# Feed-forward stage of a hybrid decoder layer: two-by-two block products with seven products in place of eight

## The chip, the core and the metric

One core of one Trainium2 chip runs the whole kernel. The metric is device time in microseconds (us), the median of the runs. TensorE does the matmuls, VectorE (DVE), ScalarE (ACT) and GpSimd (POOL) work elementwise, SyncE (SP) issues nearly all DMAs.

## What is computed

One decoder layer: a mixer (attention and a state-space part), then a gated feed-forward with a causal convolution of width 3 over the tokens. 2048 prompt tokens and 8 sample tokens; model width 1024, hidden width 2816, all float32. The part that matters:

```python
xn = rmsnorm(x, p['g_pre_ffn'])
gate = xn @ p['w_gate']
up = xn @ p['w_up']
padded = jnp.concatenate([conv_prev.astype(gate.dtype), gate], axis=1)
conv = p['conv_b'] + sum(padded[:, i:i + t] * cw[i] for i in range(CONV_W))
hdn = jax.nn.gelu(conv) * up
x = x + rmsnorm(hdn @ p['w_down'], p['g_post_ffn'])
```

## The kernel before

Stages follow each other: projections and state-space part, attention, the mixer's output projection (`stage_mix`), the feed-forward (`stage_ffn`). Each float32 matmul is made of three passes: an operand is split into a high part (a copy to type fp32r, on ScalarE, "hi") and the rest (a subtraction on VectorE, "lo"), and hi x hi, hi x lo and lo x hi are summed in PSUM. One such pass is one matmul instruction of 128x128 weights and 512 columns.

The feed-forward works on four blocks of 512 tokens (`CH`). In each block, 22 channel tiles of 128 hidden channels (`FT`) are made one after the other: `channels` (L2496) makes gate, then up, 8 slices of the model width x 3 passes = 24 matmuls each. ScalarE copies gate out of PSUM (L2647) and splits the next tile's weights (L2612); VectorE subtracts (L2705), runs the three taps (L2735, L2738), multiplies by up (L2760) and splits the hidden tile (L2765). The hidden block stays in SBUF (`hh`, `hl`). Then the block's down projection (L2598) goes over the 22 channel tiles, for four token tiles of 128 and two halves of the output width: 22 x 4 x 2 x 3 = 528 matmuls in 8 PSUM banks. The norm and the residual end each block. `w_gate` and `w_up` are read once per block, so is `w_down`. The order is written out by hand, each engine's in its own function, tied by semaphores: an engine that waits holds all that is queued behind it.

`ffn_ahead` holds the buffers that `stage_mix` fills before the feed-forward begins: x of the first block and the weights of the first tile are split there, and `ffn_first` (L2232) makes the first gate and up tile at the end of `stage_mix`. The eight sample tokens go through in the last block (L2515, L2524, L2540), beside the prompt's work.

## Time and profile before

| what | value |
|---|---|
| runs | 3451.25, 3447.12, 3445.88 us; median 3447.12 |
| profiled execution | span 3451.6 us; no time of its own is listed beside the three runs |
| mean granted TensorE clock | 0.974 |
| TensorE busy | 3242.8 us, 94% |
| VectorE, ScalarE, GpSimd busy | 2044.9, 1320.9, 603.7 us |
| HBM | 506.91 MB read, 59.30 MB written |

The feed-forward stage takes the end of the span, from 1930 us. The sum of the prediction is made against the span; the median of the runs is 4.5 us (0.13%) below it. A line such as L2496 is a line of the kernel; "idle" in a group is the time that its engine stood still just before those instructions. A matmul's mean duration is its latency: matmuls overlap, so the pace is read from counts in a window.

### The profile page before, as it was taken

The numbers are of one execution on the slowest core, as the hardware profiler recorded it, in microseconds if no ns is written. First come the engines' busy times: TensorE is split into PE (matmuls) and PEld (weight loads), VectorE is DVE, ScalarE is ACT, GpSimd is POOL, SyncE is SP. The second block draws the span as 40 slices with busy tenths as digits, with TensorE's granted clock in tenths as the row PEclk, the third lists the DMA queues.
The fourth block names the chain that finished last, engine by engine and source line by source line (L and its number), as shares of the span: only waits on it lengthen the run. The fifth ranks groups of instructions, "written<-read, shape, count | busy, mean of one in ns | idle before, by whom it ended". The sixth has DMA issues, their size and how long they took to land. (4 is left out here: it accounts for less than half of the span.)

```text
span 3451.6 us, 48037 instructions
## 1 busy us (share of the span) xinstructions
PE 3242.8 (94%) x14753; PEld 2237.2 (65%) x14753; DVE 2044.9 (59%) x2786; ACT 1320.9 (38%) x2177; POOL 603.7 (17%) x618
## 2 busy tenths in 40 slices
PE   6999885999999999998899999999999999999998
PEld 5787753444334344343788688788878887877776
DVE  6110677987988988994566555345543554255532
ACT  4100113566566556563444333223322333233321
POOL 2000101643444444441144000000000000000000
PEclk9999987999999999999899999999999999999999
DMA  3322234978988988986556333433343334344333
GB/s 116 98 79 67 77 90 111 302 239 279 303 277 284 304 276 289 306 302 235 175 167 180 99 95 109 140 110 98 97 153 105 98 98 143 101 135 122 111 118 116
DMA packets 489476, 569.78 MB, mean 165 GB/s; under 512 B 62896, under 2 KB 310800, under 8 KB 487613
## 3 DMA queue, kind: packets, MB, share of 16 engines
q1 hardware_dynamic: 482190, 551.61, 51.2%
q10 hardware_dynamic: 6912, 15.26, 1.4%
q8 instruction: 90, 1.47, 0.2%
q14 instruction: 108, 0.88, 0.1%
q0 software_dynamic: 176, 0.56, 0.1%
HBM read 506.91 MB, written 59.30 MB: 164 GB/s over the span
## 5 line engine op out<-in xcount | busy, mean ns | idle before, releaser
L2496 PE MATMUL tail_bank<-ahead_xh,ahead_wh 128*128 128x512 f32 x1392 | 547.3, 393 | 3.9 <-DVE ahead_wl L2705 2.5
L2496 PE MATMUL tail_bank<-ahead_xl,ahead_wh 128*128 128x512 f32 x1392 | 542.7, 390 | 0.0
L2496 PE MATMUL tail_bank<-ahead_xh,ahead_wl 128*128 128x512 f32 x1392 | 542.4, 390 | 0.0
L2705 DVE TENSOR_TENSOR ahead_wl<-ahead_stage,ahead_wh 128x1024 fp32r<-128x1024 f32 x173 | 211.9, 1225 | 357.2 <-ACT ahead_wh L2612 357.0
L1374 POOL TENSOR_TENSOR att_S<-att_S,att_X 128x512 f32<-128x512 f32 (+3 forms) x256 | 345.2, 1348 | 284.3 <-PE att_bank L1663 221.8
L1558 DVE TENSOR_TENSOR att_prod<-att_Kr,att_q_wide 128x1024 f32<-128x1024 f32 x256 | 325.9, 1273 | 4.9 <-DMA att_Kr<-in_cache_k_dram 4.6
L1658 PE MATMUL att_bank<-att_X,att_negtri 128*128 128x512 f32 (+3 forms) x640 | 297.2, 546 | 31.3 <-DVE att_X L1529 30.7
L1563 DVE TENSOR_REDUCE att_z_s<-att_prod 128x16 f32<-128x1024 f32 x256 | 313.2, 1224 | 8.8
L2496 PEld LDWEIGHTS tail_bank<-ahead_xh,ahead_wh 128*128 128x128 f32 x1392 | 261.7, 188 | 67.2 <-issue 11.2
L2709 DVE TENSOR_TENSOR ffn_wdl<-ahead_wdf,ffn_wdh 128x1024 fp32r<-128x1024 f32 x88 | 107.5, 1225 | 332.0 <-ACT ffn_wdh L2617 331.9
L2496 PEld LDWEIGHTS tail_bank<-ahead_xh,ahead_wl 128*128 128x128 f32 x1392 | 261.7, 188 | 55.1
L2496 PEld LDWEIGHTS tail_bank<-ahead_xl,ahead_wh 128*128 128x128 f32 x1392 | 262.0, 188 | 53.1
L1424 ACT ACTIVATE att_X<-att_bank 128x512 f32<-128x512 f32 (+2 forms) x320 | 171.1, 535 | 257.2 <-PE att_bank L1647 219.5
L1663 PE MATMUL att_bank<-att_S,att_negones 128*128 128x512 f32 (+3 forms) x576 | 257.6, 529 | 0.0
L2598 PE MATMUL tail_bank<-ffn_wdh,ffn_hh 128*128 128x512 f32 x704 | 217.7, 391 | 16.5 <-issue 8.7
L2617 ACT ACTIVATE ffn_wdh<-ahead_wdf 128x1024 fp32r<-128x1024 f32 x88 | 92.8, 1058 | 339.6 <-PE tail_bank L2598 312.0
L1432 ACT ACTIVATE att_Wt<-att_bank 128x512 f32<-128x512 f32 (+2 forms) x320 | 168.8, 527 | 127.7 <-PE att_bank L1663 127.6
L2598 PE MATMUL tail_bank<-ffn_wdh,ffn_hl 128*128 128x512 f32 x704 | 216.9, 389 | 0.0
L2598 PE MATMUL tail_bank<-ffn_wdl,ffn_hh 128*128 128x512 f32 x704 | 216.9, 389 | 0.0
L2458 POOL TENSOR_TENSOR ffn_st<-ffn_st,kept_eps 128x1 f32<-128x1 f32 x16 | 4.9, 304 | 1170.1 <-ACT ahead_stage L2691 1073.9
L1529 DVE SCALAR_TENSOR_TENSOR att_X<-att_X,att_bank 128x512 f32<-128x512 f32 (+2 forms) x320 | 190.9, 599 | 27.9 <-ACT att_X L1426 27.0
L1647 PEld LDWEIGHTS att_bank<-att_qhh,att_khl 128*128 128x128 f32 x320 | 60.9, 190 | 217.0 <-ACT att_Wt L1432 137.8
(395 smaller groups left out, 5611.3 us busy)
## 6 DMA issues: line engine op xcount, KB each, us to landing
att_Kr<-in_cache_k_dram SPq DMA_DIRECT2D x512, 256.0 KB, 3.8
att_Vr<-in_cache_v_dram SPq DMA_DIRECT2D x488, 256.0 KB, 3.8
ahead_wdf<-in_w_down_dram SPq DMA_DIRECT2D x108, 512.0 KB, 3.5
ahead_stage<-in_w_gate_dram SPq DMA_DIRECT2D x89, 512.0 KB, 3.9
ahead_stage<-in_w_up_dram SPq DMA_DIRECT2D x88, 512.0 KB, 3.9
qku_work<-in_x_prompt_dram SPq DMA_DIRECT2D x16, 512.0 KB, 4.0
norm_xr<-in_x_prompt_dram SPq DMA_DIRECT2D x16, 512.0 KB, 4.2
x_dram<-norm_y SPq DMA_DIRECT2D x16, 512.0 KB, 4.8
```

The costliest lines, as they stand in the source:

```text
L1374: pool.tensor_tensor(new[:, r:], old[:, r:], x[:, r:], ALU.add).then_inc(s_part, 1)
L1424: act.activation(x, bank[:, s % NZ, cols(s):], ACT.Exp).then_inc(e_ready, 1)
L1432: act.activation(Wt[:, u % NW, cols(u):], bank[:, u % NZ, cols(u):], ACT.Exp).then_inc(w_ready, 1)
L1529: stt(x, x, LN_TOP, z, ALU.min, ALU.max).then_inc(sp_ready, 1)
L1558: tt(pr, Kr[:, kk % KSLOTS], q_wide[:, None, :].to_broadcast([P, PP, AW]), ALU.mult).then_inc(k_used, 1)
L1563: dve.tensor_reduce(z_s[:, :, kk * PP:(kk + 1) * PP].rearrange("p h r -> p r h"), prod[:, kk % 2, :].rearrange("p (k h d) -> p k h d", k=P ...
L1658: last = pe.matmul(bank[:, u % NZ, o:], negtri[:], X[:, u % NX, o:], start=False, stop=True, skip_group_check=True)
L1663: last = pe.matmul(bank[:, u % NZ, o2:], negones[:], S[:, (u - 1) % 2, o2:], start=False, stop=True, skip_group_check=True)
L2496: mm = pe.matmul(bank[:, first + f % 2, :], w[:, j, k, :], x[:, k, :], start=(k == 0 and n == 0), stop=(k == KD - 1 and n == 2))
L2598: mm = pe.matmul(bank[:, 2 * t + c, :], x[:, f, cols], w[:, sl, c * CH:(c + 1) * CH], start=(f == 0 and n == 0), stop=(f == FT - 1 and n = ...
L2705: tt(wl[:, j], wf[:, j], wh[:, j].bitcast(F32), ALU.subtract).then_inc(w_lo[j], 1)
L2709: tt(wdl[:, f % 2, :], wdf[:, f % 2, :], wdh[:, f % 2, :].bitcast(F32), ALU.subtract).then_inc(wd_lo, 1)
```

## The change

A product of two-by-two blocks is made from seven block products in place of eight, with sums of blocks before and after.

**Gate and up.** The four weight blocks are gate and up (rows) by the two halves of the model width; the four x blocks are the halves of the model width by two halves of 512 tokens out of a pass of 1024 (`PASS`). The stage makes two passes over the 22 channel tiles, 44 tiles `g` (`LASTG`). Each makes seven products K1, K6, K2, K7, K5, K4, K3 in this order, each of 4 slices x 3 passes = 12 matmuls (L2689), into the PSUM banks A, B and C, two sets of three. K2, K7, K4 and K3 add onto what a bank holds, and wait until the sum before has been read: K2 for ScalarE's copy `m1`, K7, K4 and K3 for VectorE's sums `u2`, `u3` and `c22`. GpSimd makes four weight sums a tile (`weight_sums`), ScalarE and VectorE split seven weight operands of 512 columns a tile in place of two of 1024. The x operands of seven products, hi and lo, stay in SBUF. For pass 0 they are made at the head of the stage from `xnT` (`split_q`, operands of 128x2048); for pass 1 GpSimd's `sum_parts` sums quarters in tiles 4 to 19 and stores them to a DRAM tensor `xsum`; 28 slices are loaded and split during tile 21.

**Hidden.** For every two tiles GpSimd makes five sums of hidden blocks (`sum_h`), and seven operands are stored to the DRAM tensor `hop`, 256 KB each.

**Down.** The hidden channels are paired even and odd, the output width and the tokens halved. Seven products of eight steps each (56 steps `s`); a step is 11 pairs x 3 = 33 matmuls, and its left operand (128x1408) is loaded from `hop` and split by ScalarE and VectorE, two buffers. The right operands, 11 per product, are loaded through a ring of three buffers (`NWD`), summed by GpSimd (`sum_wd`), split (`split_wd`). VectorE and ScalarE add the products up in SBUF (`gather`, `evacuate`). Norm and residual follow in products 4 and 6.

**In `stage_mix`** x is no longer prepared, the first seven weight operands are (with GpSimd's sums), and `ffn_first` is gone.

```diff
+def weight_sums(pool, early, s, n, which):
+    wf, S, w_sum, tt = early["wf"], early["S"], early["w_sum"], pool.tensor_tensor
+    for j in which:
+if j:
+    pool.wait_ge(w_sum, n * 4 + j)
+if j == 0:
+    tt(S[:, 0], wf[:, s, A21], wf[:, s, A22], ALU.add).then_inc(w_sum, 1)
+elif j == 1:
+    tt(S[:, 1], S[:, 0], wf[:, s, A11], ALU.subtract).then_inc(w_sum, 1)
+elif j == 2:
+    tt(wf[:, s, A21], wf[:, s, A11], wf[:, s, A21], ALU.subtract).then_inc(w_sum, 1)
+else:
+    tt(wf[:, s, A12], wf[:, s, A12], S[:, 1], ALU.subtract).then_inc(w_sum, 1)
...
-        def one_block(b, last, begun=False):
-                    for n, (w, x) in enumerate(((wh, xh), (wh, xl), (wl, xh))):
-                        mm = pe.matmul(bank[:, first + f % 2, :], w[:, j, k, :], x[:, k, :],
-                                       start=(k == 0 and n == 0), stop=(k == KD - 1 and n == 2))
-                mm.then_inc(done, 1)
...
+        def product(g, k, s, first):
+            pe.wait_ge(w_lo, g * OPS + k + 1)
+            b = 3 * s + (A_B, B_B, A_B, B_B, C_B, B_B, C_B)[k]
+            if k in (K1, K6, K5):
+                at(pe, {K1: c11_ready, K6: c21_ready, K5: c12_ready}[k], g - 1)
+            else:
+                pe.wait_ge({K2: m1_ready, K7: u2_ready, K4: u3_ready, K3: c22_ready}[k], g + 1)
+            for q in range(KH):
+                if first == 0 and q == 0:
+                    pe.wait_ge(x_ready[k], 1)
+                if first == 1:
+                    pe.wait_ge(x_ready[k], 2 + q)
+                for n, (w, x) in enumerate(((0, 0), (0, 1), (1, 0))):
+                    mm = pe.matmul(bank[:, b, :], wop[:, k, w, q], xop(k, x)[:, q], start=(k in (K1, K6, K5) and q == 0 and n == 0),
+                                   stop=(q == KH - 1 and n == 2), skip_group_check=True)
+            mm.then_inc(prod, 1)
...
-                    for n, (x, w) in enumerate(((hh, wdh), (hh, wdl), (hl, wdh))):
-                        for c in range(2):
-                            mm = pe.matmul(bank[:, 2 * t + c, :], x[:, f, cols], w[:, sl, c * CH:(c + 1) * CH],
-                                           start=(f == 0 and n == 0), stop=(f == FT - 1 and n == 2))
...
+        for s in range(LASTS):
+            i, u = divmod(s, STEPS)
...
+            pe.wait_ge(a_lo, s + 1)
+            if s < 3:
+                pe.wait_ge((c11_ready, c21_ready, c12_ready)[s], LASTG - 1)
+            else:
+                at(pe, c_act, act_reads(s - 3))
+                at(pe, c_dve, dve_reads(s - 3))
+            for p in range(PAIRS_F):
+                n = i * PAIRS_F + p
+                if u == 0:
+                    pe.wait_ge(wd_lo, n + 1)
+                for q, (a, w) in enumerate(((0, 0), (0, 1), (1, 0))):
+                    mm = pe.matmul(bank[:, s % 3, :], a_op[s % 2][a][:, p, :], wd_op[:, n % NW, w, :], start=(p == 0 and q == 0),
+                                   stop=(p == PAIRS_F - 1 and q == 2), skip_group_check=True)
+                if u == STEPS - 1 and p < PAIRS_F - 1:
+                    mm.then_inc(wd_used, 1)
+            mm.then_inc(acc, 1)
...
+        def prepare(g, s, h2):
+            for j in range(2):
+                pool.wait_ge(w_loaded[j][s], h2 * 16 + 16)
+            if known(g, FT):
+                pool.wait_ge(s_made, g - FT + 1)
+            pool.wait_ge(w_lo, g * OPS - OPS + K5 + 1)
+            weight_sums(pool, early, s, g, (0, 1, 2))
+        def finish(g, s):
+            pool.wait_ge(w_lo, g * OPS + K2 + 1)
+            weight_sums(pool, early, s, g, (3,))
+        def sum_h(g, j, h2):
+            pool.wait_ge(h_ready, g)
+            e, o = conv[:, (j - 2) % 4], conv[:, (j - 1) % 4]
+            for x, a, b, op in ((0, e[:, 0:CH], o[:, 0:CH], ALU.add), (1, e[:, CH:], o[:, CH:], ALU.add),
+                                (2, e[:, 0:CH], o[:, CH:], ALU.add), (3, o[:, 0:CH], o[:, CH:], ALU.subtract)):
+                at(pool, hsum_stored[x], h2 * (32 if x == 0 else 16) - (32 if x == 0 else 16))
+                tt(hsum[:, x, :], a, b, op).then_inc(hsummed, 1)
+            pool.wait_ge(hsum_stored[0], h2 * 32 - 16)
+            tt(hsum[:, 0, :], e[:, CH:], e[:, 0:CH], ALU.subtract).then_inc(hsummed, 1)
...
+        def sum_parts(i, c):
+            n = i * 2 - 2 + c
+            pool.wait_ge(xp_loaded, n * 64 + 64)
+            for x, (o, a, b) in enumerate(((0, 1, 0), (1, 3, 1), (3, 3, 0), (2, 2, 3))):
+                if x:
+                    pool.wait_ge(xt_made, n * 4 + x)
+                tt(parts[:, o], parts[:, a], parts[:, b], ALU.subtract).then_inc(xt_made, 1)
+        def body(g, j, h2, i=None):
+            if not known(g, LASTG - 1):
+                prepare(g + 1, (j + 1) % 2, h2 + j % 2)
+            if known(g, 0, 1):
+                pool.wait_ge(x_ready[K2], 1)
+                pool.wait_ge(x_sum, 2)
+                tt(xq[:, 2], xq[:, 2], xq[:, 3], ALU.subtract).then_inc(x_t4, 1)
+            if j % 2 == 0 and not known(g, 0, 1):
+                sum_h(g, j, h2)
+            if i is not None and j % 2 == 0:
+                sum_parts(i, j // 2)
+            if not known(g, LASTG - 1):
+                finish(g + 1, (j + 1) % 2)
...
+        def body(g, f, j, h2):
+            s = j % 2
+            turn = known(g, FT - 1, FT)
+            sampled = known(g, FT - 1, LASTG - 1)
+            last = known(g, LASTG - 1)
+            for k in range(OPS):
+                if k == K1:
+                    act.wait_ge(prod, g * OPS + k + 1)
+                    at(act, c21_ready, g)
+                    if known(g, 0, 1):
+                        act.wait_ge(x_t4, 1)
+                        act.wait_ge(x_ready[K6], 1)
+                    act.activation(m1, bank[:, 3 * s + A_B, :], ACT.Copy).then_inc(m1_ready, 1)
+                    if known(g, 0, 1):
+                        split_q(K4, 2, x_t4, 1)
+                if k == K2:
+                    act.wait_ge(prod, g * OPS + k + 1)
+                    at(act, tapped, g * CW)
+                    act.activation(gbuf[:, CW - 1:CW - 1 + CH], bank[:, 3 * s + A_B, :], ACT.Copy).then_inc(c11_ready, 1)
+                if not last:
+                    split(g + 1, k, (j + 1) % 2, h2 + j % 2)
+                else:
+                    for n in ((0, 1), (2, 3), (4, 5), (6, 7), (8, 9), (10,), ())[k]:
+                        split_wd(n)
+                    if k == K2:
+                        split_a(0)
...
+            at(dve, saved, g)
+            ts(gbuf[:, 0:CW - 1], tl[:, 0:CW - 1], 1.0, None, ALU.mult).then_inc(carried, 1)
+            dve.wait_ge(carried, g + 1)
+            dve.wait_ge(c11_ready, g + 1)
...
+                dve.wait_ge(x_ready[K3], 1 + KH)
+            ts(c, gbuf[:, 0:PASS], tap(0), p[:, BIAS:], ALU.mult, ALU.add).then_inc(tapped, 1)
+            for k in (1, 2):
+                dve.wait_ge(tapped, g * CW + k)
+                stt(c, gbuf[:, k:k + PASS], tap(k), c, ALU.mult, ALU.add).then_inc(tapped, 1)
+            ts(tl[:, 0:CW - 1], gbuf[:, PASS:], 1.0, None, ALU.mult).then_inc(saved, 1)
...
+            for k in range(OPS):
+                if k in (K6, K7, K5, K4, K3):
+                    dve.wait_ge(prod, g * OPS + k + 1)
+                if k == K6:
+                    dve.wait_ge(m1_ready, g + 1)
+                    at(dve, tapped, g * CW)
+                    at(dve, saved, g)
+                    tt(t1, m1, b(B_B), ALU.add).then_inc(u2_ready, 1)
+                if k == K7:
+                    at(dve, h_ready, g)
+                    if known(g, 0, 1):
+                        dve.wait_ge(x_t4, 1)
+                    tt(up[:, CH:], m1, b(B_B), ALU.add).then_inc(u3_ready, 1)
+                if k == K5:
+                    dve.wait_ge(u3_ready, g + 1)
+                    tt(up[:, CH:], up[:, CH:], b(C_B), ALU.add).then_inc(c22_ready, 1)
+                if k == K4:
+                    dve.wait_ge(c22_ready, g + 1)
+                    tt(up[:, 0:CH], m1, b(B_B), ALU.add).then_inc(c21_ready, 1)
+                if k == K3:
+                    dve.wait_ge(u2_ready, g + 1)
+                    tt(t1, t1, b(C_B), ALU.add).then_inc(c12_ready, 1)
+                    taps(g, f, j, h2)
+                if not last:
+                    split(g + 1, k, (j + 1) % 2)
+                else:
+                    for n in ((), (0, 1), (2, 3), (4, 5), (6, 7), (8, 9), (10,))[k]:
+                        split_wd(n)
+                    if k == K7:
+                        split_a(0)
+                    if k == K3:
+                        split_a(1)
+                if k == K6 and not known(g, 0, 1):
+                    multiply(g - 1, (j - 1) % 4)
+                if k == K7 and sampled:
+                    sample_taps(g - FT + 1)
+                if k == K4 and sampled:
...
+        def load_wd(n):
+            i, p = divmod(n, PAIRS_F)
+            at(sp, wd_lo, n - NWD + 1)
+            for h, (odd, d) in enumerate(PAIRED[i]):
+                r = (2 * p + odd) * P
+                sp.dma_start(wd_raw[n % NWD][:, h], A["w_down"][0, r:r + P, d * CH:(d + 1) * CH]).then_inc(wd_loaded[n % NWD], 16)
...
+            if g == LASTG - 1:
+                sp.wait_ge(w_lo, LASTG * OPS)
+                sp.wait_ge(s_made, FT)
+                sp.wait_ge(x_ready[K3], 1 + KH)
+                for x in range(2):
+                    sp.wait_ge(hraw_stored[x], 16 * PAIRS_F)
+                for x in range(4):
+                    sp.wait_ge(hsum_stored[x], 16 * PAIRS_F * (2 if x == 0 else 1))
+                load_wd(0)
+                load_wd(1)
+                load_a(0)
+                load_wd(2)
+                load_a(1)
+                for n in range(NWD, PAIRS_F):
+                    load_wd(n)
+            if g % 2 == 0 and g:
+                store_h(g, (g - 2) % FT, g % 4, g // 2)
+            if g == FT - 1:
+                for n in range(NX):
+                    load_x(n)
+        for g in range(4):
...
+                ("hop", [OPS * T // 2, FT // 2 * P]), ("xsum", [4 * KH * P, CH])):
```

Order on VectorE, one gate/up tile before (512 tokens of gate and up, half of what a tile of the change makes):

```order
L2730 TENSOR_SCALAR ffn_gbuf<-ffn_tails 128x2
L2735 TENSOR_SCALAR ffn_conv<-ffn_gbuf,ahead_prm 128x512
L2738 SCALAR_TENSOR_TENSOR ffn_conv<-ffn_gbuf,ahead_prm,ffn_conv 128x512 x2
L2739 TENSOR_SCALAR ffn_tails<-ffn_gbuf 128x2
L2760 TENSOR_TENSOR ffn_conv<-ffn_conv,tail_bank 128x512
L2705 TENSOR_TENSOR ahead_wl<-ahead_stage,ahead_wh 128x1024
L2765 TENSOR_TENSOR ffn_hl<-ffn_conv,ffn_hh 128x512
L2705 TENSOR_TENSOR ahead_wl<-ahead_stage,ahead_wh 128x1024
```

And in the change, from the sum `u3` (L3033) of one tile to the sum `u2` (L3025) of the next:

```order
L3033 TENSOR_TENSOR gate_work<-gate_work,tail_bank 128x512
L2938 TENSOR_TENSOR ahead_wop<-ahead_S,ahead_wop 128x512
L3036 TENSOR_TENSOR gate_work<-gate_work,tail_bank 128x512
L2938 TENSOR_TENSOR ahead_wop<-ahead_wf,ahead_wop 128x512
L3039 TENSOR_TENSOR gate_work<-gate_work,tail_bank 128x512
L2984 TENSOR_SCALAR gate_work<-ffn_tails 128x2
L2995 TENSOR_SCALAR gate_work<-gate_work,ahead_prm 128x1024
L2998 SCALAR_TENSOR_TENSOR gate_work<-gate_work,ahead_prm 128x1024 x2
L2999 TENSOR_SCALAR ffn_tails<-gate_work 128x2
L2938 TENSOR_TENSOR ahead_wop<-ahead_wf,ahead_wop 128x512 x2
L3025 TENSOR_TENSOR gate_work<-gate_work,tail_bank 128x512
L2938 TENSOR_TENSOR ahead_wop<-ahead_S,ahead_wop 128x512
```

The taps, now 1024 wide, stand between the sum that ends a tile (L3039) and the sum `u2` (L3025) that the next tile's K7 waits for; the two splits behind them (L2938 x2) are those of K3 and K1.

Order on GpSimd in two tiles of gate/up (before, the engine had nothing there):

```order
L1731 TENSOR_TENSOR ahead_S<-ahead_wf 128x512
L1733 TENSOR_TENSOR ahead_S<-ahead_S,ahead_wf 128x512
L1735 TENSOR_TENSOR ahead_wf<-ahead_wf 128x512
L1737 TENSOR_TENSOR ahead_wf<-ahead_wf,ahead_S 128x512
L1731 TENSOR_TENSOR ahead_S<-ahead_wf 128x512
L1733 TENSOR_TENSOR ahead_S<-ahead_S,ahead_wf 128x512
L1735 TENSOR_TENSOR ahead_wf<-ahead_wf 128x512
L2594 TENSOR_TENSOR gate_work<-gate_work 128x512 x4
L2596 TENSOR_TENSOR gate_work<-gate_work 128x512
L1737 TENSOR_TENSOR ahead_wf<-ahead_wf,ahead_S 128x512
```

L2594 and L2596 are `sum_h`, L1737 is the fourth weight sum; it stands behind `sum_h`, and in tiles 4 to 19 behind `sum_parts` too.

Order on ScalarE in the last gate/up tile (g = 43):

```order
L2849 ACTIVATE gate_work<-tail_bank 128x512
L2814 ACTIVATE ffn_xw<-ahead_S 128x512
L2814 ACTIVATE ffn_xw<-ahead_wf 128x512
L2814 ACTIVATE ffn_xw<-ffn_stage 128x512
L2814 ACTIVATE ffn_xw<-ahead_S 128x512
L2797 ACTIVATE gate_work<-gate_work 128x1024
L2855 ACTIVATE gate_work<-tail_bank 128x512
L2814 ACTIVATE ffn_xw<-ahead_wf 128x512
L2814 ACTIVATE ffn_xw<-ffn_stage 128x512
L2822 ACTIVATE ahead_wop<-ahead_wf 128x1408
L2814 ACTIVATE ffn_xw<-ahead_S 128x512
L2814 ACTIVATE ffn_xw<-ahead_wf 128x512
```

L2814 splits right operands of down, L2797 is the gelu of tile 42, L2822 the first left operand. L2849 is the copy `m1`.

## Rows read from the trace of the kernel before

**Rows 1.** The page: span, TensorE's busy time, then GB/s in 40 equal slices of the span.

```profile
span 3451.6 us, 48037 instructions
PE 3242.8 (94%) x14753; PEld 2237.2 (65%) x14753; DVE 2044.9 (59%) x2786; ACT 1320.9 (38%) x2177; POOL 603.7 (17%) x618
GB/s 116 98 79 67 77 90 111 302 239 279 303 277 284 304 276 289 306 302 235 175 167 180 99 95 109 140 110 98 97 153 105 98 98 143 101 135 122 111 118 116
```

**Rows 2.** Windows: matmuls of L2496 alone; window, length, PE busy, PEld busy, granted clock, DMA.

```profile
2380.00:2500.00 120.00, 120.00 (x531) 99.36 (x530) 1.00 0.33 97
```

**Rows 3.** The page's groups of instructions: matmuls; out<-in, shapes, count, busy us, mean ns, idle.

```profile
L2496 PE MATMUL tail_bank<-ahead_xh,ahead_wh 128*128 128x512 f32 x1392 | 547.3, 393 | 3.9 <-DVE ahead_wl L2705 2.5
L2598 PE MATMUL tail_bank<-ffn_wdh,ffn_hh 128*128 128x512 f32 x704 | 217.7, 391 | 16.5 <-issue 8.7
```

**Rows 4.** The same groups from 1960 us on: TensorE's work for the eight sample tokens.

```profile
L2515 PE MATMUL tail_bank<-ahead_stage,ffn_xs 128*32 128x256 f32 (+1 forms) x352 | 24.3, 396 | 5.6 <-issue 5.0 <-DVE ffn_hs L2757 0.6
L2524 PE MATMUL tail_bank<-kept_sel,ffn_s_rows 128*128 128x8 f32 x88 | 11.2, 237 | 0.0
L2540 PE MATMUL tail_bank<-ahead_wdf,ffn_hs 128*32 128x512 f32 x80 | 10.7, 605 | 0.0
```

**Rows 5.** Waits of TensorE from 1930 us on: total, times, longest.

```profile
PE tail_bank L2598 <- issue: 8.7, 4, 2.6
PE tail_bank L2598 <- DVE ffn_wdl L2709: 7.7, 3, 3.1
```

**Rows 6.** Timeline of TensorE, 1920 to 1940 us: start, duration, instruction, idle time before.

```profile
1920.33 1.02 PE L2190 MATMUL tail_bank<-kept_ident,norm_xn 8*128 8x8 f32 x8 [2.56 <-DVE norm_xn L2166]
1925.29 0.63 PE L2232 MATMUL tail_bank<-ahead_xh,ahead_wh 128*128 128x512 f32 x1
1925.72 0.63 PE L2232 MATMUL tail_bank<-ahead_xl,ahead_wh 128*128 128x512 f32 x1
1930.69 0.47 PE L2496 MATMUL tail_bank<-ahead_xh,ahead_wh 128*128 128x512 f32 x1 [1.13 <-PEq L63]
1938.91 0.50 PE L2496 MATMUL tail_bank<-ahead_xh,ahead_wh 128*128 128x512 f32 x1 [2.50 <-DVE ahead_wl L2705]
```

**Rows 7.** Timeline of the DMA queue: the last issue of the stage before the feed-forward.

```profile
1921.70 0.37 SPq L1956 DMA_DIRECT2D xnT_dram<-norm_xt  x1
```

**Rows 8.** Timeline of VectorE within one gate tile.

```profile
2418.15 0.55 DVE L2735 TENSOR_SCALAR ffn_conv<-ffn_gbuf,ahead_prm 128x512 f32<-128x512 f32 x1 [0.28 <-DVE ffn_gbuf L2730]
2418.85 0.75 DVE L2738 SCALAR_TENSOR_TENSOR ffn_conv<-ffn_gbuf,ahead_prm,ffn_conv 128x512 f32<-128x512 f32 x1 [0.15 <-DVE ffn_conv L2735]
2422.16 1.22 DVE L2705 TENSOR_TENSOR ahead_wl<-ahead_stage,ahead_wh 128x1024 fp32r<-128x1024 f32 x1 [0.26 <-ACT ahead_wh L2612]
```

**Rows 9.** Groups from 1960 us on: an addition that reads PSUM, and ScalarE's split and PSUM copy.

```profile
L2760 DVE TENSOR_TENSOR ffn_conv<-ffn_conv,tail_bank 128x512 f32<-128x512 f32 x85 | 58.4, 687 | 37.8 <-ACT ffn_conv L2651 37.8
L2612 ACT ACTIVATE ahead_wh<-ahead_stage 128x1024 fp32r<-128x1024 f32 x168 | 176.0, 1048 | 0.0
L2647 ACT ACTIVATE ffn_gbuf<-tail_bank 128x512 f32<-128x512 f32 x85 | 51.0, 600 | 309.2 <-PE tail_bank L2496 309.2
```

**Rows 10.** GpSimd: one group by form; then a stretch of the timeline where it meets VectorE.

```profile
L1374 POOL TENSOR_TENSOR att_S<-att_S,att_X 128x512 f32<-128x512 f32 x168 | 264.9, 1577 | 284.3 <-PE att_bank L1663 221.8 <-DVE att_X L1529 62.6
...
1855.36 1.81 POOL L2023 TENSOR_TENSOR norm_sq<-norm_sq 128x512 f32<-128x512 f32 x1
1856.32 1.92 DVE L2107 TENSOR_TENSOR norm_mixl<-norm_mix,norm_mixh 128x1024 fp32r<-128x1024 f32 x1 [0.31 <-ACT norm_mixh L2050]
1857.24 1.60 POOL L2025 TENSOR_TENSOR norm_sq<-norm_sq 128x256 f32<-128x256 f32 x1
```

**Rows 11.** DMA issues of the page: KB each, median us from issue to landing.

```profile
ahead_stage<-in_w_gate_dram SPq DMA_DIRECT2D x89, 512.0 KB, 3.9
```

**Rows 12.** Timeline, the end: TensorE's last matmuls and the last addition.

```profile
3438.02 0.61 PE L2598 MATMUL tail_bank<-ffn_wdh,ffn_hl 128*128 128x512 f32 x2
3445.90 1.22 DVE L2801 TENSOR_TENSOR ahead_wdf<-ffn_sums,ahead_wdf 128x1024 f32<-128x1024 f32 x1
```

1140 lines of the change are left out of this document (613 added, 527 removed).

## The prediction, made before the changed kernel was run

> **What bounds the kernel now.** I read the page first, then windows and groups, then waits, then the timeline. TensorE is busy 94% of the span [rows 1]. From 1930 us on it is the bound: in a window of 120 us within gate and up it never stands still, at full granted clock, and makes 531 matmuls [rows 2], so one costs 120/531 = 0.226 us (the 0.39 us of its groups is latency, [rows 3]). Its waits in the whole stage are few: 8.7 and 7.7 us before the down matmuls [rows 5]. So a matmul that is left out is worth 0.226 us, as long as the other engines keep up, and the question is whether they do.
>
> **What is removed.** Gate and up took 4 x 22 x 48 = 4224 matmuls (three groups of 1392 and the first tile's 48, [rows 3]), and take 44 x 84 = 3696. Down took 3 x 704 = 2112, and takes 56 x 33 = 1848. The difference is 792, times 0.226 = 179 us. Shapes and columns stay the same. Weights are read twice, not four times; a 512 KB load lands in 3.9 us [rows 11], and per pair of tiles the new stage moves 2 MB of weights, 1.75 MB of `hop` and about 1 MB of x quarters in 38 us, 125 GB/s, well below the 300 GB/s that the page's slices show in attention [rows 1]. I cost the bytes at nothing; if a load is late it stands in the terms below.
>
> **The head of the stage.** Before, the last projection work hid x and the first tile. Now nothing of x can be loaded until `stage_mix` ends. Its last store is issued at 1921.7 [rows 7]; with a landing like that of a small transfer (under 3.9 us) and the 1.1 us which TensorE idled between the stages [rows 6], the new stage starts at about 1926. Then four loads of 1 MB: at 300 GB/s 3.4 us each, the first lands at +4.5, the last at +16. Operands of 2048 columns cost twice the rows for 1024: ScalarE 2.1 us [rows 9], VectorE 2.4 us [rows 8]. VectorE has K1's lo, a sum, the lo of K3 and K2 (+20.6, behind the last load), a second sum (23), then K6's lo behind ScalarE (27.5). So TensorE makes K1 at about +10 and K6 only at +27; three more lo parts, one weight split and `u2` put K7 at +35, and four products of 12 x 0.226 = 2.7 us follow: tile 0 is done at +46, at 1972 us. The bounds are 1962 (GpSimd and landings hidden) and 1987 (GpSimd's two 2048-wide sums at four times the 1.58 us of [rows 10] each in the chain).
>
> **A steady tile.** 84 x 0.226 = 19.0 us; 43 tiles are 816 us. VectorE per tile: 7 splits and 5 PSUM sums at 0.69 [rows 9], taps and product of 1024 columns at 1.08, 1.28, 1.28 and 1.22 (from 0.55, 0.75 and the 1024-wide split, [rows 8]; slopes of 0.53 us per 512), small ones 0.3: 13.5 us, and ScalarE about 6.6. Both fit in 19. But order matters. With time 0 at K1: K3 of the tile before has just ended (0.2), VectorE sums (0.9), carries two columns (1.3), runs three taps with the 0.15 to 0.28 us between dependent ones [rows 8] (5.7), splits K3 and K1 (7.0), and only then makes `u2` (7.8). K7 should start at 3 x 2.72 = 8.2. The margin is 0.4 us. `u3` and `c22` have 1.8 us.
>
> Two things eat that margin. First, GpSimd: an addition of 512 columns takes 1.58 us on average [rows 10], and where it meets VectorE both stretch: 1.92 in place of 1.22 for VectorE, 1.60 for GpSimd's 256 columns [rows 8, 10]. Per two tiles it has 8 weight sums and 5 hidden sums, 13 x 1.58 = 20 us of 38: it fits, but after `sum_h` the next tile's first three sums fall on the taps. Second, in tiles 4 to 19 the order weight sums, `sum_h`, `sum_parts`, fourth sum is serial: the product of the even tile is ready at 9, five sums end at 16 to 17, only then SP issues the loads of the quarters (land at 20.5), four sums of 256 (23.8), fourth weight sum (25.1). ScalarE waits for that in its split of K3, in front of `m1`: `m1` comes at 26.4, K2 should start at 24.5. So about 2.8 us for each odd tile of pass 0 (10 of them, 28 us) and 0.9 us for each of pass 1 (11, 10 us): **38 us**. The bounds are 0 (margins hold) and 120 us (below).
>
> The same lines as rule: the Trainium skill, SBUF — State Buffer, section Who interferes with whom, says that VectorE and GpSimd share a port pair as an exclusive lock, and that a VectorE instruction with two SBUF inputs fully blocks behind a GpSimd one that reads SBUF. The rows of the stretched pair agree in direction. By it both wide taps could each lose a whole GpSimd addition in every tile; that is the second rival, and speaks against this change.
>
> **Turn, transition, down.** In tile 21, 28 slices of x are split besides: 28 x 0.69 = 19 us more on VectorE, 33 in all against 19, of which about 9 can be taken from later slack (K7 of tile 22 starts at 35 and not at 27): **10 us** (0 to 19). In the last tile ScalarE's order has right operands of down before the gelu, and they come through a ring of three: load 3.5 to 3.9 us [rows 11], sum 1.3 to 1.6 [rows 10], hi and lo 0.6 and 0.7. SP may load only when tile 43's splits are done (+6), so ScalarE stands until about +12, VectorE reaches `u3` at +21 where K4 wanted it at +13.6, and the eleventh operand comes at about +42, when step 0 should have ended at +26.5: **20 us** with a slow clock behind it (bounds 5 and 35). Down itself is 1848 x 0.226 = 418 us; a step is 7.5 us, in which VectorE has a split of 1408 (1.7), one or two sums, 1.4 small splits and at most a norm and residual (2.5): under 6, hidden. **4 us** for waits where a product's last three right operands turn over (before, down waited 16 us in all, [rows 5], which bounds it). The sample tokens' work stays: 24.3 + 11.2 = 35 us in gate/up, 10.7 and some tails, 15 us, in down [rows 4]. After the last matmul: a sum 0.7, square 1.2, root 0.8, scale 1.3, add 1.2, store; the present end takes 3451.6 - 3438.6 = 13 us [rows 12], I take 10.5.
>
> **Sum:** 1972 + 816 + 35 + 38 + 10 + 20 + 418 + 15 + 4 + 10.5 = 3338.5 us of span, 113 below 3451.6. The median stands 4.5 below its span, so **3334 us**.
>
> **The rivals.**
> *Clean.* Margins hold, and the loads' latency is hidden: the 72 us of stalls are gone, 3262 us. For it: the trace shows loads landing early and few waits [rows 5, 11]. Against: three separate margins of about a microsecond. With half of the stalls, 3298.
> *GpSimd sets the chain.* Both wide taps wait a whole GpSimd addition (2 x 1.58) in every tile, `u2` comes at 11.0, 2.8 us late: 43 x 2.8 = 120 in place of 38, 3416 us. For it: the stretched pair [rows 10]. Against: only odd tiles have the sums there by my order.
> *Slow clock, slower than before.* Behind an idle of 2.56 us, twelve matmuls ran 0.43 us apart and not 0.226 [rows 6]: 2.4 us more, TensorE at the lower of its two levels. If every tile has a stall of 2.5 us and this tail, it is 4.9 x 43 = 211 in place of 38, 3507 us. It beats the gain from (3447 - 3334 + 38)/43 = 3.5 us a tile. Against: my stalls are shorter. I give it 8%.
> *Even.* Stalls of just this size, or products that are not paced as now: within 0.2% of before, which is about what a measurement can tell; 2%.
>
> **How the numbers follow.** Forecast 60%, clean 12%, GpSimd chain 18%, slow clock 8%, even 2%. The range runs from 3280 (half way into clean) to 3430 (the GpSimd chain with its 14 us of room); outside lie slow clock, even, and half of clean. Faster: 60 + 12 + 18 = 90%; same 2%; slower 8%.
>
> **What would show it.** In the new trace: L2689 with 3696 matmuls and down with 1848, at 0.226 us in windows without waits; the first K6 about 27 us after the stage's start; in odd tiles 5 to 19 TensorE idle before K2 for ScalarE's copy, and ScalarE idle before K3's split for L1737; TensorE idle before K7 for L3025; a gap of over 5 us in tile 43 and another in step 0. Wrong would be: windows in mid-stage with less than 80 matmuls per 19 us and no wait named (the clock), waits for DMA at L2689, or down steps far over 7.5 us.

## The result and the profile after

The changed kernel takes 3461.9 us (median of 19 runs, 3453.08 to 3472.53) against 3451.15 us (19 runs) for the kernel before in the same session: ratio 1.003, 95% interval 1.0021 to 1.0039. It is 0.3% slower. The prediction said 3334 us, with a range up to 3430: wrong in size and in direction. The profiled execution has a span of 3457.6 us and took 3459.6 us; the sum of the prediction stood at 3338.5 us of span, so 119 us are to be explained.

The page of the changed kernel, the lines that answer to [rows 1] and [rows 3]:

```profile
span 3457.6 us, 47005 instructions
PE 3148.2 (91%) x13945; PEld 2115.6 (61%) x13945; DVE 2335.3 (68%) x2904; ACT 1323.6 (38%) x2249; POOL 1179.2 (34%) x996
...
L2689 PE MATMUL tail_bank<-ffn_xw,ahead_wop 128*128 128x512 f32 x2112 | 530.4, 409 | 72.9 <-DVE ffn_xw L2943 31.6
L2766 PE MATMUL tail_bank<-ffn_xw,ahead_wop 128*128 128x512 f32 x1848 | 451.0, 405 | 20.8 <-DVE ahead_wop L2957 17.6
L2689 PE MATMUL tail_bank<-gate_xr,ahead_wop 128*128 128x512 f32 x1584 | 381.6, 399 | 16.2 <-DVE gate_work L3030 11.5
```

The counts are the announced ones: 2112 + 1584 = 3696 and 1848, 792 fewer than before. TensorE's busy time fell only by 95 us, from 3242.8 to 3148.2, where 792 x 0.2267 us are 180 us. And it now waits, where it had hardly waited [rows 5]. Waits of TensorE in the changed kernel from 1900 us on (total us, times, longest):

```profile
PE tail_bank L2689 <- DVE ffn_xw L2943: 31.6, 2, 17.8
PE tail_bank L2689 <- ACT gate_work L2849: 27.9, 8, 4.3
PE tail_bank L2766 <- DVE ahead_wop L2957: 17.6, 7, 4.4
PE tail_bank L2689 <- DVE gate_work L3030: 11.5, 2, 10.5
PE tail_bank L2689 <- DVE gate_work L3025: 8.9, 1, 8.9
...
PE tail_bank L2724 <- ACT down_C L2911: 7.4, 1, 7.4
```

The places are found in the timeline of TensorE, changed kernel (start, duration, instructions, idle before):

```profile
1936.91 5.46 PE L2689 MATMUL tail_bank<-ffn_xw,ahead_wop 128*128 128x512 f32 x12 [13.75 <-DVE ffn_xw L2943]
1960.21 7.18 PE L2689 MATMUL tail_bank<-ffn_xw,ahead_wop 128*128 128x512 f32 x24 [17.84 <-DVE ffn_xw L2943]
1979.25 2.03 PE L2689 MATMUL tail_bank<-ffn_xw,ahead_wop 128*128 128x512 f32 x8
...
2184.05 8.56 PE L2689 MATMUL tail_bank<-gate_xr,ahead_wop 128*128 128x512 f32 x36
2192.45 5.76 PE L2689 MATMUL tail_bank<-ffn_xw,ahead_wop 128*128 128x512 f32 x24
2201.55 7.42 PE L2689 MATMUL tail_bank<-ffn_xw,ahead_wop 128*128 128x512 f32 x24 [3.33 <-ACT gate_work L2849]
2208.80 8.56 PE L2689 MATMUL tail_bank<-gate_xr,ahead_wop 128*128 128x512 f32 x36
...
2433.15 3.33 PE L2689 MATMUL tail_bank<-ffn_xw,ahead_wop 128*128 128x512 f32 x7 [8.88 <-DVE gate_work L3025]
...
2926.78 5.46 PE L2689 MATMUL tail_bank<-gate_xr,ahead_wop 128*128 128x512 f32 x12 [10.51 <-DVE gate_work L3030]
...
2967.18 1.02 PE L2724 MATMUL tail_bank<-kept_ident,ffn_tails 128*10 128x128 f32 x4 [7.38 <-ACT down_C L2911]
...
3009.65 50.56 PE L2766 MATMUL tail_bank<-ffn_xw,ahead_wop 128*128 128x512 f32 x216
...
3268.86 1.65 PE L2766 MATMUL tail_bank<-ffn_xw,ahead_wop 128*128 128x512 f32 x3 [4.31 <-DVE ahead_wop L2957]
```

Two things are read here. First the **pace**: 36 matmuls from 2184.05 to 2192.45 without a gap, 8.40/36 = 0.2333 us each, at a granted clock of 1.00 (window 2184 to 2192); down has the same (216 in 50.56 us: 215 distances and the last one's 0.4 us). In the kernel before it is 0.2267 us: the window of [rows 2] counts 531, of which about 1.7 belong to its edges, 120/529.3. Over 5544 matmuls that is 5544 x 0.0066 = 37 us. Nothing waits there: it is a slower TensorE at the same clock, and no row of waits would show it. Second the **gaps**, and behind each a tail: the 24 matmuls after the gap at 2201.55 take 7.25 us to the next start where 24 took 5.6, 1.65 us more: the granted clock is 0.58 of full speed in the first 3.5 us of them and 0.94 in the next 4, so a part of them ran at the lower of the two levels, as in [rows 6].

Term by term against the prediction's sum (span; the tiles and steps are measured between the first matmuls of each):

| term | predicted | measured | |
|---|---|---|---|
| tile 0 done | 1972 | 1979.2 | +7 |
| 43 tiles of 84 matmuls | 816 | 843 | +27 |
| samples in gate/up (tiles 20 to 42) | 35 | 35 | 0 |
| odd tiles 5 to 19, over 19.6 each | 38 | 43 | +5 |
| turn (tiles 21, 22: 36.4 + 26.8, usual 21.2) | 10 | 21 | +11 |
| tile 43 (37.8, usual 19.6) and steps 0 to 2 (39.0, usual 23.1) | 20 | 34 | +14 |
| down, 1848 matmuls | 418 | 431 | +13 |
| samples and tails in down | 15 | 22 | +7 |
| waits in down's other steps (25 of standing still, the rest a slower pace, most of it behind the stops) | 4 | 38 | +34 |
| end | 10.5 | 10.6 | 0 |

The right column adds up to 118 of 119 us. From its first matmul to the end of the span the stage takes 1520.7 us, against 1520.9 before (from 1930.69, [rows 6]). The kernel before had 48 of its gate/up matmuls behind it at that point, so this stretch lost 744 matmuls, 169 us, and all of it came back; the span is 6 us longer since the first matmul comes 6 us later.

The gaps have their releasers on other engines. The odd tile at 2201.55, changed kernel, timelines of GpSimd and ScalarE:

```profile
2187.58 1.30 POOL L2596 TENSOR_TENSOR gate_work<-gate_work 128x512 f32<-128x512 f32 x1
2193.90 5.23 POOL L2605 TENSOR_TENSOR ffn_stage<-ffn_stage 128x256 f32<-128x256 f32 x4 [5.02 <-DMA ffn_stage<-xnT_dram]
2199.09 1.26 POOL L1737 TENSOR_TENSOR ahead_wf<-ahead_wf,ahead_S 128x512 f32<-128x512 f32 x1
...
2200.38 0.63 ACT L2786 ACTIVATE ahead_wop<-ahead_wf 128x512 fp32r<-128x512 f32 x1 [9.89 <-POOL ahead_wf L1737]
2200.91 0.58 ACT L2849 ACTIVATE gate_work<-tail_bank 128x512 f32<-128x512 f32 x1
```

GpSimd has ended `sum_h` at 2188.9, stands 5.0 us for quarters of x, sums them, and only then makes the fourth weight sum, to which ScalarE's split is tied, and behind that split stands the copy `m1` that K2 waits for: the chain that the prediction wrote down. At the turn, in the step after the transition and in down, the same kernel's ScalarE and SP:

```profile
2423.57 2.44 SPq L2454 DMA_DIRECT2D gate_work<-xnT_dram  x4
2429.03 2.65 ACT L2793 ACTIVATE ffn_xw<-gate_work 128x512 fp32r<-128x512 f32 x4 [9.28 <-DMA gate_work<-xnT_dram]
...
2951.84 6.70 SPq L2417 DMA_DIRECT2D hop_dram<-gate_work  x7
2959.14 0.93 SPq L2474 DMA_DIRECT2D ahead_wf<-hop_dram  x2
2965.28 1.38 ACT L2822 ACTIVATE ahead_wop<-ahead_wf 128x1408 fp32r<-128x1408 f32 x1 [14.24 <-DMA ahead_wf<-hop_dram]
...
3253.97 0.60 SPq L2524 DMA_DIRECT2D out_y_prompt_dram<-down_C  x1
3256.14 0.48 SPq L2462 DMA_DIRECT2D ahead_S<-in_w_down_dram  x1
3262.86 0.63 ACT L2814 ACTIVATE ffn_xw<-ahead_S 128x512 fp32r<-128x512 f32 x1 [7.13 <-DMA ahead_S<-in_w_down_dram]
```

In all three ScalarE stands at the head of its queue for a load that SP issued late. At the turn SP has the load of x behind the weights' loads, which it may issue only when their buffer is free; after the transition it has the left operand's behind seven stores; in down it has the right operand's behind the store of y, which waits for the norm. That is what the runs below had to test.

### The profile page after: what moved, and what is told of

Same layout as the page of the kernel before. It is cut to its first block and busy times, and to the rows that moved or that the text cites. A ratio compares the mean times of both kernels' runs of the same rounds, so it can differ in the third digit from the quotient of the medians.

```text
span 3457.6 us, 47005 instructions
## 1 busy us (share of the span) xinstructions
PE 3148.2 (91%) x13945; PEld 2115.6 (61%) x13945; DVE 2335.3 (68%) x2904; ACT 1323.6 (38%) x2249; POOL 1179.2 (34%) x996
## 5 line engine op out<-in xcount | busy, mean ns | idle before, releaser
L2689 PE MATMUL tail_bank<-ffn_xw,ahead_wop 128*128 128x512 f32 x2112 | 530.4, 409 | 72.9 <-DVE ffn_xw L2943 31.6
L2689 PEld LDWEIGHTS tail_bank<-ffn_xw,ahead_wop 128*128 128x128 f32 x2112 | 408.1, 195 | 182.0 <-issue 50.3
L2766 PE MATMUL tail_bank<-ffn_xw,ahead_wop 128*128 128x512 f32 x1848 | 451.0, 405 | 20.8 <-DVE ahead_wop L2957 17.6
L2766 PEld LDWEIGHTS tail_bank<-ffn_xw,ahead_wop 128*128 128x128 f32 x1848 | 354.7, 193 | 121.1 <-DVE ahead_wop L2957 20.7
L2689 PE MATMUL tail_bank<-gate_xr,ahead_wop 128*128 128x512 f32 x1584 | 381.6, 399 | 16.2 <-DVE gate_work L3030 11.5
L2689 PEld LDWEIGHTS tail_bank<-gate_xr,ahead_wop 128*128 128x128 f32 x1584 | 300.4, 190 | 90.3 <-issue 18.1
L2786 ACT ACTIVATE ahead_wop<-ahead_wf 128x512 fp32r<-128x512 f32 x215 | 135.2, 629 | 318.6 <-PE tail_bank L2689 218.6
L2938 DVE TENSOR_TENSOR ahead_wop<-ahead_wf,ahead_wop 128x512 fp32r<-128x512 f32 x215 | 179.5, 850 | 39.3 <-ACT ahead_wop L2786 37.6
L1667 PEld LDWEIGHTS att_bank<-att_S,att_negones 128*128 128x128 f32 x576 | 112.2, 195 | 121.3 <-issue 106.5
L1430 ACT ACTIVATE att_X<-att_X 128x512 f32<-128x512 f32 (+2 forms) x320 | 181.3, 567 | 10.1
L2594 POOL TENSOR_TENSOR gate_work<-gate_work 128x512 f32<-128x512 f32 x88 | 129.1, 1495 | 138.0 <-DVE gate_work L2964 138.0
L1682 PE MATMUL att_bank<-att_Wt,att_vh 128*64 128x512 f32 (+3 forms) x640 | 161.1, 560 | 6.8 <-ACT att_Wt L1436 6.8
```

The costliest lines, as they stand in the source:

```text
L1430: act.activation(x, x, ACT.Ln, bias=1.0).then_inc(l_ready, 1)
L1667: last = pe.matmul(bank[:, u % NZ, o2:], negones[:], S[:, (u - 1) % 2, o2:], start=False, stop=True, skip_group_check=True)
L2689: mm = pe.matmul(bank[:, b, :], wop[:, k, w, q], xop(k, x)[:, q], start=(k in (K1, K6, K5) and q == 0 and n == 0), stop=(q == KH - 1 and n ...
L2766: mm = pe.matmul(bank[:, s % 3, :], a_op[s % 2][a][:, p, :], wd_op[:, n % NW, w, :], start=(p == 0 and q == 0), stop=(p == PAIRS_F - 1 and ...
L2938: tt(wop[:, k, 1], weight_part(early, k, s), wop[:, k, 0].bitcast(F32), ALU.subtract).then_inc(w_lo, 1)
```

## The experiments

The theory: (1) the pace comes from where the two operands lie in SBUF; (2) the odd tiles from GpSimd's order; (3) turn, transition and down from the order of SP's issues and of ScalarE's splits. By the buffers' start addresses in bytes in the program as compiled, the gate/up operands of the kernel before both begin at 480 modulo 512, those of down both at 224; in the changed kernel x begins at 416 and the weights at 480. The rival to (1) is that the new form of the products (accumulation into shared banks, more distinct operands, busier VectorE and GpSimd) slows TensorE. Totals of single runs carry up to 14 us of difference from the stages before; so where one part is judged I use the **stage length**, from K1's first matmul (1936.9 in the changed kernel) to the first matmul of the last step of down (3439.3): 1502.4 us there. It repeats within 1 us in the two pairs of kernels that should have the same stage (1486.3 and 1485.5, 1408.4 and 1408.9). `a_align` has ten runs, `b_shift`, `c_both`, `d_all` and `d_pads` have four each, the others one.

**1. Align the operands: `a_align`.**

```diff
+        m.sb("pad", [P, 16])
         xw = m.sb("xw", [P, 4, 2, KH, CH], F32R)
```

> The changed kernel with 64 bytes of padding in front of its x operands, so that every matmul's two SBUF operands start at the same offset modulo 512 bytes (480 and 480 in place of 416 and 480). Address theory: the changed kernel's matmuls, 233.3 ns apart in the mean and never settled, go back to the 226.7 ns of the kernel before; 5544 matmuls x 6.6 ns = 36.6 us less, about 3425 us. Rival, waits at every product keep TensorE's queue short: 233 ns stays, no change in time.

3442.33 us (10 runs; ratio to the kernel before 0.9975, 0.9965 to 0.9985), stage 1486.3. Timeline of TensorE:

```profile
2210.30 7.34 PE L2690 MATMUL tail_bank<-ffn_xw,ahead_wop 128*128 128x512 f32 x24 [4.40 <-ACT gate_work L2850]
2217.48 8.32 PE L2690 MATMUL tail_bank<-gate_xr,ahead_wop 128*128 128x512 f32 x36
2225.64 11.04 PE L2690 MATMUL tail_bank<-ffn_xw,ahead_wop 128*128 128x512 f32 x48
...
3009.82 50.48 PE L2767 MATMUL tail_bank<-ffn_xw,ahead_wop 128*128 128x512 f32 x222
```

36 matmuls in 8.16 us, 0.2267: the old pace, from 64 B. The time fell by 20 us and the stage by 16, not by 37. The gap before K2 grew from 3.3 to 4.4 us: an even and an odd tile of pass 0 take 44.3 us together as before, so their length is the GpSimd chain's, not TensorE's, and about 9 us are lost there. Down gave 7 us and not 12, as its stops grew too.

**2. The same, by the other operand: `a_wop64`** (a pad of 64 B before `wop`; both then at 416).

> The changed kernel with its weight operands moved down by 64 bytes, so both operands lie at 416 modulo 512. If only the difference of the two addresses counts: 226.7 ns apart and about 37 us less, as with the other padding. If the place of the moving operand itself counts: 233 ns and no change. If waits count: no change.

3445.33 us (one run), stage 1485.5, the same 8.16 us for 36 matmuls. With both operands at 480 or both at 416 the pace is the same: what counts in these two is how far one lies from the other.

**3. The reverse, in the kernel before: `b_shift`** (`wh`, `wl` moved by 64 B, `hh`, `hl` by 128 B).

> The kernel before with its gate/up weight operands moved by 64 bytes against x, and the hidden operands of down moved by 128 bytes against the weights of down; nothing else. Address theory: gate/up matmuls 233.3 ns apart, 4224 x 6.6 = 28 us more; down 14 us more if 128 bytes count too (the projection's matmuls at the kernel's start, whose operands are 128 bytes apart modulo 256, run at 232 to 233 ns), so 28 or 42 us more, 3479 to 3493 us. Rival, waits: no change, 3451 us.

3468.69 us (4 runs; ratio 1.0055, 1.0037 to 1.0072): 19 us slower with not an instruction changed. Gate/up go at 0.2301 us, down at 0.2324 (means of the intervals under 0.3 us). From the first gate/up matmul of `stage_ffn` to the last of down it is 23.8 us longer (1507.6 to 1531.4). Less than the expected 28 to 42: at 64 B this code loses half of what the changed kernel lost. The two differ in sign: in the changed kernel the moving operand (x) begins 64 B below the weights, here 64 B above them.

**4. 256 B, 32 B, and matmuls that the change left alone: `b_256`** (kernel before; `wh` by 256 B, `hh` by 32 B, and the mixing stage's `mixh`, `mixl` by 448 B, from 64 B beside their weights to none).

> The kernel before with the gate and up weights moved by 256 B against x, down's hidden operands by 32 B against its weights, and the mixing stage's activations by 448 B, which makes them equal to their weights modulo 512. If the pace repeats with 256 B, gate and up stay at 226.7 ns; if it repeats only with 512 B, they go to 230 or more (1392 x 3 matmuls, about +14 us). Down at 32 B: if any difference costs, about 230 to 232 ns. The mixing stage goes from 233 to 227 ns (5 us) if the rule holds outside the feed-forward stage.

3463.8 us (one run). Windows of gate/up and down (L2499 and L2601 alone), then two starts in the mixing stage:

```profile
2380.00:2500.00 120.00, 120.00 (x531) 99.36 (x530) 1.00 0.33 97
3330.00:3380.00 50.00, 50.00 (x216) 40.27 (x216) 1.00 0.28 90
...
1867.62 0.39 PE L2207 MATMUL tail_bank<-mix_woh,norm_mixh 128*128 128x512 f32 x1
1871.02 0.39 PE L2207 MATMUL tail_bank<-mix_woh,norm_mixh 128*128 128x512 f32 x1
```

Gate/up at 256 B: 531 in the window of [rows 2], as before. So the pace repeats with 256 B, and the "modulo 512" of my expectations is too coarse. Down at 32 B: 216 in 50 us, 0.2333. And 15 matmuls of the mixing stage take 3.40 us. The same places in the kernel before, the window of down (L2598 alone) and the timeline:

```profile
3330.00:3380.00 50.00, 50.00 (x223) 41.39 (x222) 1.00 0.30 98
```

```profile
1867.63 0.40 PE L2205 MATMUL tail_bank<-mix_woh,norm_mixh 128*128 128x512 f32 x1
1871.14 0.39 PE L2205 MATMUL tail_bank<-mix_woh,norm_mixh 128*128 128x512 f32 x1
```

There it is 223, and 3.51 us. The form of the products is not needed for it: theory (1) stands, for several pairs of buffers and in both directions.

**5. GpSimd's order: `a_finish`** (changed kernel; the fourth weight sum before the sums of the parts).

```diff
-                    if i is not None and j % 2 == 0:
-                        sum_parts(i, j // 2)
                     if not known(g, LASTG - 1):
                         finish(g + 1, (j + 1) % 2)
+                    if i is not None and j % 2 == 0:
+                        sum_parts(i, j // 2)
```

> The changed kernel with GpSimd's fourth weight sum in front of the four sums of x quarters, not behind them. Chain theory: ScalarE no longer waits for it before its copy of K1; the 3.4 to 4.4 us of idle TensorE before K2 in tiles 5, 7, ... 19 go, and the slow clock behind each: 8 x 5.1 = 41 us less, about 3421 us. Rival, VectorE and GpSimd meet on the taps: u2 stays late, the idle time moves to K7, less than 15 us.

3433.36 us (one run), stage 1470.4, 32 us less. Odd tiles take 20.6 us instead of 24.7, and the gap before K2 is gone. The timeline of TensorE in an odd tile shows K7 and K4 with the rest:

```profile
2193.38 3.04 PE L2689 MATMUL tail_bank<-ffn_xw,ahead_wop 128*128 128x512 f32 x12 [0.21 <-DVE gate_work L3025]
2196.26 2.96 PE L2689 MATMUL tail_bank<-gate_xr,ahead_wop 128*128 128x512 f32 x12
2199.55 5.84 PE L2689 MATMUL tail_bank<-gate_xr,ahead_wop 128*128 128x512 f32 x24 [0.33 <-DVE gate_work L3030]
```

9 of the expected 41 us did not come: each odd tile is still 1.0 us over an even one, with short waits for VectorE's `u2` and `u3`.

**6. Both: `c_both`** (pad and order).

> Both edits together: the operands of the gate and up products moved by 64 B so that x and weights lie at the same address modulo 512, and GpSimd's fourth weight sum ahead of the sum of the parts. If pace and the chain in odd tiles of pass 0 are two independent costs, both now come back: the pair of a tile and the next in pass 0 goes from 44.3 us to about 19.1 + 20.1 = 39.5 us (8 pairs, -38 us), the other 27 tiles go from 84 x 0.2333 = 19.6 to 19.1 us (-13 us), and down gives back up to 1848 x 0.006 = 11 us less what its other chains take. Against the changed kernel -55 to -62 us, median about 3400 us, 1.5% faster than before. If the alignment only moved time into waits for good (as in the run with the alignment alone, where 19 of 37 us showed), the sum is -31 -19 = -50 us or less: 3412 us.

3405.15 us (4 runs; ratio 0.9875, 0.9849 to 0.9902), stage 1451.0: 51.4 us less, while the two alone gave 16.1 + 32.0 = 48.1. Even tiles take 19.0 us, odd ones of pass 0 20.9, with waits of 0.2 us before K7 and 1.2 before K4. The two causes are separate, and the alignment gives more once TensorE is the bound again.

**7. Loads before a store: `a_la`** (`c_both`, and `load_a(2)`, `load_a(3)` issued ahead of the last `store_h`).

> As the run with both edits (pace and sum order), and only the third and fourth left operands of down loaded before the last hidden slice is stored. If ScalarE stands in its split for a load that SP issues behind that store, the 9.2 us for which TensorE stands before the tail product of step 1 go, and the time falls by 8 us against the run with both edits; if the wait has another cause, such as the copy of the tails itself, it stays as it is.

3413.63 us, one run, which by itself would say that it costs 8 us; but its stage begins at 1948.6 and that of `c_both` at 1934.2. The stage takes 1445.0, 6.0 less, and step 1 takes 9.3 us in place of 17.8. What the late load cost is shown; a little of it comes back in steps 2 and 3 (10.1 and 9.6 in place of 9.5 and 8.0).

**8. The order of the last tile: `c_last`** (`a_la`, and in tile 43 the gelu, its products and sums ahead of the splits of down's operands).

```diff
-                            for n in ((0, 1), (2, 3), (4, 5), (6, 7), (8, 9), (10,), ())[k]:
+                            if k == K7:
+                                split_a(0)
+                            for n in ((), (), (0,), (1, 2), (3,), (4, 5), (6,))[k]:
                                 split_wd(n)
...
```

> As the run before, and with two edits about the transition: the third and fourth left operands of down are loaded before the last hidden slice is stored, and in the last tile ScalarE and VectorE do the gelu chain and its products before the splits of down's operands. If the order of those engines is what makes tile 43 long (TensorE stands 10.9 us before K4 and 3.9 us before K3) and the late load is what holds step 1 (7.8 us before its tail product), tile 43 goes from 37.8 to about 24 us, steps 0 to 2 from 11.0, 17.5, 10.5 to 14 (the operands of down come later now), 8.5 and 8.5 us: together from 77 to about 55 us, -22 us. If the ring of three weight tiles and its loads set the pace whatever the order, the gaps move from tile 43 into step 0 and only the 7.8 us go.

3391.62 us (one run), stage 1436.9. Tile 43 takes 19.0 us, not a stop in it, in place of 38.6; but step 0 grows from 10.1 to 27.9. Tile 43 and steps 0 to 2: 76.0 in `c_both`, 68.9 in `a_la`, 64.2 here, so 12 less and not 22, and only 5 of them from the order. Timelines of this kernel, TensorE and GpSimd in step 0:

```profile
2889.35 1.65 PE L2769 MATMUL tail_bank<-ffn_xw,ahead_wop 128*128 128x512 f32 x3 [4.55 <-DVE ffn_xw L2958]
...
2886.90 1.77 POOL L2641 TENSOR_TENSOR ffn_stage<-ffn_stage 128x512 f32<-128x512 f32 x1 [1.75 <-DMA ffn_stage<-in_w_down_dram]
```

The eleven right operands now pass through the ring of three in step 0, pair by pair, load, sum, split; the rival named in the expectation is largely right: the ring sets most of the length, the order mainly where it is paid.

**9. The turn: `c_turn`** (`c_both`, and x's operands for pass 1 split later, the last three products' in tile 22).

> As the run with both edits, and the x operands of pass 1 split later at the turn: two products' worth stay in tile 21 ahead of their use, three move into tile 22. If VectorE's and ScalarE's own load of 28 extra splits sets the length of tiles 21 and 22 (36.4 + 26.8 us for the two in the changed kernel, 21 us too many), spreading does not help much: -3 us. If it is that ScalarE stands before the weights' split of K7 for an x slice whose DMA was issued late (9.3 us), the gap of 9.1 us before K7 goes: tiles 21 and 22 together from 63 to 50 us, -10 to -13 us against the run with both edits.

3399.46 us (one run), stage 1443.6, 7.4 less, 5.9 of them in tiles 21 and 22. The stop of 9.1 us before K7 of tile 21 is gone (that tile takes 23.3 us in place of 36.8); tile 22 takes 35.2 in place of 27.6, with stops of 6.0 us before K7 and some 3.5 before K4. ScalarE's timeline in tile 22:

```profile
2410.48 1.30 ACT L2795 ACTIVATE gate_xr<-gate_work 128x512 fp32r<-128x512 f32 x2 [4.96 <-DMA gate_work<-xsum_dram]
```

Again it stands for an x slice: in part the wait moved with the splits. The expected 10 to 13 us were too much.

**10. Down's loads one step earlier: `c_loads`** (`c_both`; of the eleven right operands of each next product the first five are loaded one step earlier).

```diff
-                    for n in ops_of(s, 8, 8):
+                    for n in loads_of(s):
                         load_wd(n)
...
```

> As the run with both edits, and the right operands of down loaded one step earlier. If the gaps of TensorE in down at steps 16, 17, 25, 32, 37 to 42 and 48 (about 40 us in all) come from loads that SP issues late, behind a store that waits, they shrink to under 15 us in all: -20 us or more. If they come from the work of VectorE at the turnover (norm, residual and splits in one step), they stay: within 5 us of the run with both edits.

3385.18 us (one run), stage 1425.9, 25.1 less: the largest gain in down. Steps 36 to 41 take 46.8 us in place of 70.4; the long steps 16, 31 and 47 stay. The waits of TensorE for VectorE's left operands in down, here and in `c_both`:

```profile
PE tail_bank L2775 <- DVE ahead_wop L2966: 5.7, 4, 3.2
```

```profile
PE tail_bank L2767 <- DVE ahead_wop L2958: 21.1, 7, 5.6
```

TensorE waited for VectorE by the profile, yet in these steps VectorE's work was not the cause: ScalarE, which feeds it, stood for a load behind a store that waits for the norm.

**11. All of it: `d_all`.**

> All the edits tried so far in one kernel: operands at the same address modulo 512, the fourth weight sum before the sum of parts, the early loads of down's third and fourth left operands, the order of the last tile, the later splits of x at the turn, and down's right operands loaded one step earlier. If the costs are separate, against the run with the first two (3405 us) it gains what each showed alone: the loads of down 20 us, the last tile 12 to 14 us, the turn 6 us, together about 40 us: 3363 us, 2.4% faster than before. If they share one chain (SP's queue or VectorE's work, so that a wait removed in one place stands again in the next) it comes to 3375 us or more.

3371.53 us (4 runs; ratio 0.9759, 0.9738 to 0.9781), stage 1408.4. The single gains (7.4, 14.1 for the last tile with the early loads, 25.1) would give 1404.4, so nearly all of it adds up.

**12. And the stages before: `d_pads`** (`d_all`, a pad of 448 B before `mixh` and of 384 B before the projection's weights).

> As the run with all edits, and two more pads in stages that the change does not touch: the mixing stage's activations and the projection's weights are moved so that both operands of those matmuls lie at the same address modulo 512 (before: 64 B and 128 B apart, at 233.2 and 232.6 ns a matmul). If the pace depends on the difference of the two addresses, the mixing matmuls (about 800) fall to 227 ns, the first two token chunks of the projection too, and the kernel gains 5 to 8 us more against the run with all edits. If the pace of those stages has another cause (other shapes of access, or the address has nothing to do with it there), they stay at 233 and the time at that of the run with all edits.

3361.23 us (4 runs; ratio 0.9739, 0.9721 to 0.9756); the intervals of `d_all` and `d_pads` overlap, so the step between them is shown by the pace alone. The mixing stage goes from 233.2 to 227.7 ns. In the projection the first two token chunks, now equal to the weights modulo 256, go from 232.5 and 232.8 to 227.8 and 227.4 ns (means of the intervals under 0.245 us, the first tile of channels left out); the other two, whose rows are 1032 floats long and so move by 32 B with every slice, were at 232.7 and 232.5 and are at 232.0 and 232.6. It is the fastest version, 2.6% under the kernel before.

## Why the prediction was wrong, point by point

**"Shapes and columns stay the same", so 0.226 us a matmul.** This step failed, and with it 40 of the 119 us (27 in the tiles, 13 in down; 4 of the 40 are 0.226 in place of 0.2267). Columns and shapes did stay; the addresses did not. Runs 1 to 4 show that 64 B do it. In the prediction's own sum that is 40 us, but to give the old pace back alone was worth less: `a_align` takes 3442.33 us, still outside the range, as the stops took part of it. The signs that I named for a wrong pace were too coarse for it: less than 80 matmuls per 19 us, where 0.2333 us give 81.

**"4 us for waits" in down.** 38 us. I bounded them by the 16 us of [rows 5], which belong to a loop with other loads, and counted VectorE's work in a step (under 6 of 7.5 us), never SP's: the right operands of the next product are issued after x, the `hop` slice and the store that waits for the norm, and ScalarE waits in order. Run 10 shows it: 25 us back from the order of the issues alone. So two terms failed most, the price of a matmul and these waits: 40 and 34 of the 119 us.

**Odd tiles.** The mechanism is the one foreseen, GpSimd's serial order up to `m1`, and run 5 removes it. The sizes were off both ways: 8 tiles and not 10, 5.4 us each and not 2.8 (3.5 of waiting, the rest for the most part at the lower clock), nothing in pass 1 where 10 were put. 43 for 38: the sum came out near since the errors cancel, which was luck.

**Turn.** 21 for 10, just over the bound of 19. I counted splits, but ScalarE stood 9.3 us for a load issued behind the weights'. Run 9 removes 5.9 us of the two tiles. The 10 had a slip as well: the 9 us of slack are taken from the 19 us of added splits, while VectorE's 33 us stand over a tile of 19 by 14 only.

**Transition.** 34 for 20, inside the bounds of 5 to 35. The ring of three and ScalarE's order were named; the 7.4 us in step 1, a left operand loaded only after seven stores, were not (run 7).

**Head, samples, end.** K1 came at 1936.9 (predicted about 1936) and K6 23.3 us later where 17 were reckoned; tile 0 was done 7 us late, which I have not tested. Samples in gate/up and the end came out exactly; in down they cost 22 us for 15.

**The rivals.** *Clean* is refuted. *GpSimd sets the chain* had the stretched VectorE right. The group of the second and third taps in the changed kernel, tiles 1 to 42:

```profile
L2998 DVE SCALAR_TENSOR_TENSOR gate_work<-gate_work,ahead_prm 128x1024 f32<-128x1024 f32 x84 | 150.1, 1787 | 6.5 <-DVE gate_work L2995 0.2 <-DVE gate_work L2998 0.2
```

The 1.79 us are a mean of three cases. 27 of the 84 took 1.28 us, as I had reckoned, all but one of them with GpSimd idle; 15 took 1.53 to 1.57, beside its sums of 256 columns; 42, two in nearly every tile from the turn on, took 2.20 beside its weight sums of 512 columns, and those sums took up to 2.16 in place of 1.30. Taps on VectorE and sums on GpSimd, changed kernel, without and with each other:

```profile
2219.48 2.71 DVE L2998 SCALAR_TENSOR_TENSOR gate_work<-gate_work,ahead_prm 128x1024 f32<-128x1024 f32 x2
2214.60 1.30 POOL L1733 TENSOR_TENSOR ahead_S<-ahead_S,ahead_wf 128x512 f32<-128x512 f32 x1
...
2479.37 4.44 DVE L2998 SCALAR_TENSOR_TENSOR gate_work<-gate_work,ahead_prm 128x1024 f32<-128x1024 f32 x2
2480.57 2.16 POOL L1733 TENSOR_TENSOR ahead_S<-ahead_S,ahead_wf 128x512 f32<-128x512 f32 x1
```

So the rival's condition, that both taps are held up in every tile, was true of nearly all of pass 1, and what was wrong in it was the price: 0.92 us a tap and not 1.58. TensorE waited for `u2` only once, at the turn. In tile 2 `u2` ends 6.5 us after K1's first matmul, where I had reckoned 7.8, and in the tiles of pass 1 it ends at 8.24 us and K7 starts at 8.87: the slower taps fit into what I had put too high elsewhere. The Trainium skill, SBUF — State Buffer, section Who interferes with whom, calls the pair of ports that the two engines share an exclusive lock. Of a VectorE instruction with two SBUF inputs it says that it contends with a GpSimd one that reads SBUF; the words "fully blocks", which the prediction took over, stand there for VectorE's two-port modes. The lock agrees with this case in direction (the two do hold each other up), but a tap loses 0.92 us here, not a whole sum of 1.30. Its cost showed only once the rest was fast: run 6 leaves 1.9 us per odd tile of pass 0. *Slow clock* had the mechanism but not the places: 1.65 us behind each stop, in 8 tiles, not in 43. *Even* named products that are not paced as now, at 2%, without a cause or a price. The result, slower than before, was reached by none of the ways that I priced, and it took three kinds of cost at once.

## What to carry to other kernels

When a change moves buffers, check first that both SBUF operands of every hot matmul still begin at the same address modulo 256; a pad of 64 bytes decides 3% of the matmul time here, and no wait shows it, only the distance between starts. Count the queues like engines: for each operand of each step ask behind which store its load is issued, and whether that store waits; an engine named by a wait is often only the last link behind a late load. And judge a part by the length of its own stage, since single totals moved by 14 us with the stages ahead.

## What the runs showed of the hardware

- The pace of 512-column fp32r matmuls depends on the difference of the start addresses of their two SBUF operands, modulo 256 B: 226.7 to 227.7 ns at 0 (also at 256 B), 233.2 to 233.3 ns at 32 B and in the mixing stage and the changed kernel at 64 B, 230.1 at 64 B in `b_shift`'s gate/up, 232.4 at 128 B in its down. Where 64 B cost 6.6 ns the moving operand begins 64 B below the other (modulo 256), in three loops; where they cost 3.4 it begins 64 B above. That the sign decides is not shown, since no run changes it within one loop; other differences weren't tried. The Trainium skill, SBUF — State Buffer, section Who interferes with whom, gives TensorE two read ports on SBUF, one for the moving operand and one for the weights, and calls them independent. Taken alone, that leaves no reason for the distance of the two to matter; these runs show that it does, and the measurement decides. By what mechanism they meet isn't shown.
- Behind a stop of 3.33 us (2201.55, changed kernel) 24 matmuls take 7.25 us in place of 5.6, at a mean granted clock of 0.77. The stop costs 5 us in all.
- VectorE's taps of 1024 columns take 1.28 us alone, 1.53 us beside GpSimd's sums of 256 columns and 2.20 us beside those of 512, which themselves take 2.16 us in place of 1.30: there each engine loses about 0.9 us per instruction.
